# Score matmuls of a dilated attention: the keys of a query tile taken as all 1,024, or as own half, adjoining tile and every fourth key of the other half

## What is computed

```
DIL_BRANCHES = ((128, 1), (512, 4), (2048, 16))      # (window, dilation)
off  = kk[None, :] - half - qq[:, None]              # within one residue class
mask = abs(off) <= half  and  0 <= key_pos < L
out  = sum over branches of softmax(lse) * branch_out
```

## Time and profile before

| | |
|---|---|
| median of three runs | 3317.93 us |
| the profiled execution | 3315.9 us |
| its span in the trace | 3313.9 us |
| TensorE matmul busy | 3197.8 us, 96% |
| TensorE weight loads busy | 2720.6 us, 82% |
| VectorE busy | 1555.4 us, 47% |
| ScalarE busy | 936.2 us, 28% |
| GpSimd busy | 901.0 us, 27% |

### The profile page before, as it was taken

How to read it: one execution, slowest core, us unless ns; L and a number is a source line. 1 busy time by engine, 2 the same in 40 slices (tenths; PEclk the granted TensorE clock), 3 DMA queues, 4 the chain that set the end, 5 groups by cost and what they waited for, 6 DMA issues and landing times.

```text
span 3313.9 us, 42751 instructions
## 1 busy us (share of the span) xinstructions
PE 3197.8 (96%) x17492; PEld 2720.6 (82%) x17492; DVE 1555.4 (47%) x3160; ACT 936.2 (28%) x1814; POOL 901.0 (27%) x570
## 2 busy tenths in 40 slices
PE   8999999999999999999989999999999999999997
PEld 7888887888888888888778888878888888888886
DVE  6866757262333333332668667572523333333336
ACT  4433434441111111111344334444411111111112
POOL 2111112653222222222441111125522222222224
PEclk9999999999999999999989999999999999999999
DMA  3111011231111111110321110021311111111112
GB/s 143 40 56 51 20 36 64 93 127 45 39 39 39 39 39 39 39 39 32 133 72 44 53 51 20 35 82 75 127 51 39 39 39 39 38 37 36 38 56 103
DMA packets 50481, 184.27 MB, mean 56 GB/s; under 512 B 8048, under 2 KB 11760, under 8 KB 46832
## 3 DMA queue, kind: packets, MB, share of 16 engines
q1 hardware_dynamic: 47984, 173.68, 15.2%
q10 hardware_dynamic: 2304, 7.87, 0.6%
HBM read 144.81 MB, written 28.84 MB: 52 GB/s over the span
## 4 chain that ended last, share of the span: by engine, by line
PE 81%; DVE 10%; DMA 3%; issue 2%; ACT 1%; SPq 1%; POOL 1%; DVEq 0%; POOLq 0%; ACTq 0%
PE PS L1739 25%; PE PS L1741 24%; PE PS L1740 24%; PE PS L1882 3%; PE PS L1851 3%; PE PS L1866 2%; DVE PT L1507 1%; SPq L624 1%; DVE XL L1350 1%; DVE ACC L1343 1%; DMA SW<-Rq 1%; DVE SW L1400 1%; DVE YO L1343 1%; DVE ACC L1346 1%; DVE YO L1346 1%
## 5 line engine op out<-in xcount | busy, mean ns | idle before, releaser
L1739 PE MATMUL PS<-XH,WH 128*128 128x512 f32 (+1 forms) x3648 | 1327.7, 364 | 21.7 <-DVE XL L1358 5.7
L1741 PE MATMUL PS<-XH,WL 128*128 128x512 f32 (+1 forms) x3648 | 1300.6, 357 | 0.0
L1740 PE MATMUL PS<-XL,WH 128*128 128x512 f32 (+1 forms) x3648 | 1300.3, 356 | 0.0
L1739 PEld LDWEIGHTS PS<-XH,WH 128*128 128x128 f32 x3648 | 693.5, 190 | 147.4 <-issue 21.4
L1741 PEld LDWEIGHTS PS<-XH,WL 128*128 128x128 f32 x3648 | 692.4, 190 | 101.8
L1740 PEld LDWEIGHTS PS<-XL,WH 128*128 128x128 f32 x3648 | 693.5, 190 | 93.0
L794 POOL TENSOR_TENSOR WL<-RAW,WH 128x1024 fp32r<-128x1024 f32 x196 | 468.9, 2411 | 960.8 <-ACT WH L965 960.8
L817 POOL TENSOR_TENSOR SG<-SG,RS 128x512 f32<-128x512 f32 x132 | 147.9, 1121 | 997.5 <-ACT SG L1104 997.5
L1579 DVE TENSOR_TENSOR ACC<-ACC,PS 128x512 f32<-128x512 f32 (+1 forms) x480 | 286.3, 598 | 246.4 <-PE PS L1741 245.1
L1739 PE MATMUL PS<-HH,WH 128*128 128x512 f32 (+1 forms) x1056 | 379.2, 359 | 11.9 <-DVE ACC L1579 10.4
L1741 PE MATMUL PS<-HH,WL 128*128 128x512 f32 (+1 forms) x1056 | 378.7, 359 | 0.0
(11 more groups left out here) (118 smaller groups left out, 2859.8 us busy)
## 6 DMA issues: line engine op xcount, KB each, us to landing
RAW<-w_in SPq DMA_DIRECT2D x48, 512.0 KB, 3.5
RAW<-w_gate SPq DMA_DIRECT2D x44, 512.0 KB, 3.5
RAW<-w_up SPq DMA_DIRECT2D x44, 512.0 KB, 3.5
RAW<-w_down SPq DMA_DIRECT2D x44, 512.0 KB, 3.7
X<-parked SPq DMA_DIRECT2D x6, 2048.0 KB, 7.8
RAW<-w_out SPq DMA_DIRECT2D x16, 512.0 KB, 4.2
parked<-YO SPq DMA_DIRECT2D x4, 2048.0 KB, 6.5
mixed<-YB ACTq DMA_DIRECT2D x8, 640.0 KB, 2.9
```

The lines of the kernel that those rows point to most:

```text
L1739: nc.tensor.matmul(out, wh, xh, start=first, stop=False)
L1740: nc.tensor.matmul(out, wh, xl, start=False, stop=False)
L1741: return nc.tensor.matmul(out, wl, xh, start=False, stop=last)
```

## The change

The scores of a sample pair are computed in three parts instead of two quads: the 512 keys of the query's own half, the 128 keys of the adjoining tile of the other half, and the 128 stepped keys of the other half (same residue r as the queries, moving operand with a step of 4 elements). The second and third part share bank 2h + 1. The 512 columns of one bank and 256 of the next are all that is computed. The table masks, in the adjoining tile, the keys whose distance is a multiple of 4, since those are among the stepped ones; the stepped part has no key masked for being near. The two VectorE instructions now take 512 and 256 (two pieces of 128) numbers. The order of the value tiles follows: own half, adjoining tile, stepped. The table LOG grows by 6 columns. Prompt tiles and the neighbourhood blocks are as before.

```diff
-DIL_UNITS = [(i, h, 3 * (i // 4), 6) for i in range(8) for h in range(2)] + \
+DIL_UNITS = [(i, h, 4 * (i // 4), 6) for i in range(8) for h in range(2)] + \
...
-NEAR = HALF_S + P
-LOG_STEPPED = (P + 3 + NEAR, P + 3 + NEAR + P)
+LOG_BESIDE = (HALF_S + 3, HALF_S + 3 + P + 3)
+LOG_STEPPED = (LOG_BESIDE[1] + P + 3, LOG_BESIDE[1] + P + 3 + P)
...
-    near = np.arange(P + 3 + NEAR)[None, :] - P - 3 - STEP * q
-    far = [np.arange(P)[None, :] + first for first in (P, -P)]
-    stepped = [np.where((k < P + P // STEP) & (k >= -P // STEP), f(MASKED), log_count(STEP * (k - q))) for k in far]
+    own = np.arange(HALF_S + 3)[None, :] - 3 - STEP * q
+    beside = [np.arange(P + 3)[None, :] - 3 + first - STEP * q for first in (HALF_S, -P)]
+    stepped = [STEP * (np.arange(P)[None, :] + first - q) for first in (P, -P)]
     prompt = np.arange(3 * P)[None, :] - P - q
-    log = np.concatenate([log_count(near)] + stepped + [log_count(prompt)], 1)
+    log = np.concatenate([log_count(own)] + [np.where(d % STEP, log_count(d), f(MASKED)) for d in beside]
+                         + [log_count(d) for d in stepped] + [log_count(prompt)], 1)
...
-            if b not in DIL or i >= 8 or a < 5:
+            if b not in DIL or i >= 8 or a < 4:
                 return V[:, k0 + a, h, :]
             half, r = half_of(i)
+            if a == 4:
+                return V[:, 4 - half, h, :]
             return VS[0][:, r, h, :] if half == 0 else VS[1 + r // 2][:, r % 2, h, :]
...
-                    at = (P if half == 0 else 0) + 3 - r
-                    nc.vector.tensor_tensor_reduce(PR[:, u % 2, 0:NEAR], ps[:, 3 * P * half:3 * P * half + NEAR],
-                                                   LOG[:, at:at + NEAR], -1.0, 3e38, ALU.add, ALU.min,
-                                                   NM_NEAR[:, n:n + 1]).then_inc(s_near, 1)
-                    dve.wait_ge(s_near, 16 * (DIL[-1] + 1) * L + 16 * b + u + 1)
-                    nc.vector.tensor_tensor_reduce(PR[:, u % 2, NEAR:NEAR + P], stepped(ps, 1 - half, r),
-                                                   LOG[:, LOG_STEPPED[half]:LOG_STEPPED[half] + P], -1.0,
-                                                   NM_NEAR[:, n:n + 1], ALU.add, ALU.min,
+                    low, high = LOG_BESIDE[half] + 3 - r, LOG_STEPPED[half]
+                    nc.vector.tensor_tensor_reduce(PR[:, u % 2, 0:HALF_S], ps[:, 0:HALF_S],
+                                                   LOG[:, 3 - r:3 - r + HALF_S], -1.0, 3e38, ALU.add, ALU.min,
+                                                   NM_OWN[:, n:n + 1]).then_inc(s_own, 1)
+                    dve.wait_ge(s_own, 16 * (DIL[-1] + 1) * L + 16 * b + u + 1)
+                    other = slice(HALF_S, HALF_S + 2 * P)
+                    tab = LOG[:, low:2 * high - low].rearrange("p (m n) -> p m n", m=2)[:, :, 0:P]
+                    nc.vector.tensor_tensor_reduce(PR[:, u % 2, other].rearrange("p (m n) -> p m n", m=2),
+                                                   ps[:, other].rearrange("p (m n) -> p m n", m=2),
+                                                   tab, -1.0, NM_OWN[:, n:n + 1], ALU.add, ALU.min,
                                                    NM[:, n:n + 1]).then_inc(s_masked, 1)
...
-                    halves = b in DIL and i < 8
-                    if halves:
-                        k0, nkt = 0, 2 * STEP
+                    if b in DIL and i < 8:
+                        scores_halves(pair)
+                        return
...
+                def scores_halves(pair):
+
+                    half, r = half_of(units[2 * pair][0])
+                    for part, (bank, at, n) in enumerate(((0, 0, HALF_S), (1, 0, P), (1, P, P))):
+                        for m, (q, k) in enumerate(((QH, KH), (QH, KL), (QL, KH))):
+                            keys = (k[:, HALF_S * half:HALF_S * half + HALF_S],
+                                    k[:, (4 - half) * P:(5 - half) * P], stepped(k, 1 - half, r))[part]
+                            for h in range(2):
+                                own = slice(HD * h, HD * h + HD)
+                                last = nc.tensor.matmul(PS[:, 2 * h + bank, at:at + n],
+                                                        stepped(q, half, r)[own, :], keys[own, :],
+                                                        start=m == 0, stop=m == 2)
+                                if m == 2 and part == 2:
+                                    last.then_inc(s_scored, 1)
```

More of the change, by code:

```diff
@@ L438, in build @@
         STAT = place("STAT", [P, 16], offset=base + 97920)
-        NM, SM, NM_NEAR, CW = STAT[:, 0:4], STAT[:, 4:8], STAT[:, 8:12], STAT[:, 12:15]
+        NM, SM, NM_OWN, CW = STAT[:, 0:4], STAT[:, 4:8], STAT[:, 8:12], STAT[:, 12:15]
         YS = place("YS", [P, 2, P], offset=base + 97984)
@@ L491, in build @@
         s_masked = sem("masked")
-        s_near = sem("near")
+        s_own = sem("own")
         s_exped = sem("exped")
@@ L1849, in scores @@
                                 own = slice(HD * h, HD * h + HD)
-                                qs = stepped(q, *half_of(i)) if halves else q[:, i * P:(i + 1) * P]
-                                last = nc.tensor.matmul(PS[:, 2 * h + a // 4, 0:n * P], qs[own, :], k[own, keys],
+                                last = nc.tensor.matmul(PS[:, 2 * h + a // 4, 0:n * P],
+                                                        q[own, i * P:(i + 1) * P], k[own, keys],
                                                         start=m == 0, stop=m == 2)
                                 if m == 2 and a + n == nkt:
+                                    last.then_inc(s_scored, 1)
[11 more added lines that the diff above has]
+                                if m == 2 and part == 2:
                                     last.then_inc(s_scored, 1)
```

## The result

The changed kernel takes 3338.39 us (median of four runs, 3334.35 to 3340.21) against 3316.91 us of the kernel before: a ratio of 1.0066, 95% interval 1.0049 to 1.0084, so slower by 0.66%, 21.5 us. Predicted were 3333 us, +15. The two profiled spans are 3313.9 and 3335.5 us, 21.6 apart.

A forecast was written before the change was run, and what follows sets the result against it. TensorE was taken as the bound: 3315.9 us profiled, +16.3 for 33 pairs on the chain, +1 for 15 others, -1 for VectorE, gave 3332.2, so a median near 3333 us. Likeliest range 3328 to 3341 us; 8 in 10, 3319 to 3350.

The forecast's parts named there:

- The bound: In the stretches with dilated blocks, TensorE sets the time, busy 317.80 of 329 and 321.91 of 336 us.
- 6 x 0.22 = +1.32 us: On TensorE, six new 128-column steps per sample pair, each at the pace of a stepped-query load, 0.22 us.
- The end of the pair: On TensorE, last matmul start to next group's load shrinks from 0.33 to 0.21 us: -0.12 us a pair.
- 33 of the 48 sample pairs set the end: Pairs on TensorE's part of the chain, each 0.495 us longer: 33 x 0.495 = +16.3 us.
- On the 15 others a longer pair first uses up the wait that follows: Pairs off TensorE's chain: mean wait of 0.86 us absorbs most of the 0.495 us each, leaving +1 us.
- some 12: TensorE's waits for PT low in the dilated stretches were to shrink from 18 us to some 12.
- 814 + 351 ns become about 681 + 410 ns: VectorE's two masking instructions: -0.074 us a unit, -7.1 us over 96, of which -1 us counts on the chain.
- the step cost 77 ns, which is the whole gain: Bound for VectorE's masks: if two pieces cost as much extra as the step does now, nothing is saved.
- (a): Rival: stepped loads on TensorE keep up at 0.11 us, so the kernel gets faster, 3310.5 us; chance 0.10.
- (b): Rival: stepped keys fight the loads for SBUF, +1.26 us a pair, 3366 us; chance 0.14.
- (c): Rival: VectorE's slack absorbs TensorE's extra time, at most 10.4 us through the waits, near 3322 us; chance 0.14.
- half-way, 3345 us: Mark given under the rival of stepped keys fighting loads, between the forecast and that rival's 3366 us.

The follow-up runs named there:

- run 8: Changed kernel with the part over the adjoining tile done twice, same result: 3366.04 us, ratio 1.0154 to the kernel before.
- run 4: Changed kernel with the dilated blocks' queries stored by residue, so a query tile is plain, same result: 3313.26 us, 0.9989 of the kernel before.
- run 6: Changed kernel with queries stored by residue and the second mask as one run of 256 numbers (wrong table): 3315.06 us, 1.0000 of the kernel before.
- run 9: Changed kernel with queries stored by residue, repeated with more executions: 3314.54 us, 0.9995 of the kernel before.
- run 1: Changed kernel with plain queries in sample pairs, stepped keys kept (other scores): 3312.67 us, 0.9987 of the kernel before.
- run 2: Changed kernel with plain keys in the third part, queries still stepped (other scores): 3334.26 us, 1.0054 of the kernel before.
- run 5: Changed kernel with the second masking instruction as one run of 256 numbers instead of two pieces (wrong table): 3339.34 us, 1.0071 of the kernel before.
- run 11: Changed kernel with the second mask's minimum started from a constant, not the first one's result: 3340.28 us, 1.0071 of the kernel before.
- run 3: Changed kernel with both queries and third-part keys plain (other scores): 3313.53 us, 0.9992 of the kernel before.
- run 7: Kernel before, still in two quads, with only its dilated blocks' queries stored by residue: 3314.29 us, 0.9998 of the kernel before.
- the three-part form with residues: Changed kernel with the dilated blocks' queries written side by side by residue: 3313.26 us (0.9989 of the kernel before), again 3314.54 us (0.9995).

## Why the prediction was right, step by step

**The bound.** TensorE leads in these stretches: right. Extra time on it shows at 37.7 us for each us of a pair (21.5 / 0.57), and 39.5 to 42 for the next 0.70 us (run 8). Cutting it pays less: from the kernel before down to 1.56 us it is 0.17 us a pair for 0 to 4 us (runs 4, 6 and 9), 0 to 22 us for each us.

**What a short step costs.** The mechanism was right: a 128-column matmul cannot hide a load of stepped queries. Runs 1 and 2 settle it, since plain queries take the whole loss away and plain keys almost nothing. The loads of the short steps are 0.233 us apart. But the six steps together took less than "6 x 0.22 = +1.32 us": from the start of the last long matmul, 86.76, to that of the last short one, 88.00, it is 1.24 us, since the second short matmul is put only 0.06 us behind the first.

**The end of the pair** was the term that was off: "-0.12 us", a last start to next load of 0.21 us read from a pair with plain queries. It measured 0.36 us after, 0.33 with plain keys. A load that is exposed between short steps is exposed at the end too. The two sizes err in opposite ways, -0.08 us for the six steps and +0.15 for the end, so a pair grew by 0.57 us instead of 0.495. That the sum is so near is in part luck. Counted by loads: from the first to the last it is 1.85 us where it was 1.17, three loads more, +0.68, and from the last to the next group's 0.45 us where it was 0.56, -0.11. With plain keys a pair is 0.04 us shorter (run 2); the rest is the slow loads.

**The pairs that count.** "33 of the 48 sample pairs set the end" held for the kernel before. "On the 15 others a longer pair first uses up the wait that follows" was priced at 1 us; 10 of the 15 came onto the chain, and one of the 33 left it. 33 x 0.57 = 18.8 us, 42 x 0.57 = 23.9; measured 21.5, between. TensorE's waits for PT low and the sums are 15.3 us in 19, after 18.0 in 21, but over windows 39 us longer in all. Over the same work (80 to 421 and 1746 to 2087 us) they are 13.8 us in 17, still more than "some 12".

```profile
PE PS L1902 <- DVE PT L1512: 6.2, 7, 2.1
...
PE PS L1911 <- DVE YS L1486: 1.2, 2, 0.6
```

Those two lines are TensorE's waits in layer 0, 80 to 425 us, against the earlier trace rows; in layer 1, 1745 to 2100 us, they are 5.4 and 2.5 us.

**VectorE.** "814 + 351 ns become about 681 + 410 ns" was wrong, though its bound ("the step cost 77 ns, which is the whole gain") has the measured value. The reason given for the bound is wrong too: 484 ns stays in one piece (run 5) and falls to 425 with a constant start (run 11). The second mask of the kernel before has such a start as well, so of the 77 ns that the prediction gave to the step some 59 are likely the start and 18 the step (an estimate from run 11). The gain was priced at 1 us, and the time shows nothing of it (run 11).

**The rivals.** (a), loads at 0.11 us in short steps, is what plain queries do and stepped ones don't. The figure of 81 ns in the Trainium skill, "TensorE: Matmul & The Clock Gate", section on the back-to-back issue gap, is not reached here even with both operands plain: the loads of run 3 are 0.11 us apart. There two loads and two matmuls, one for each head, run side by side; but the transposes, single 128x128 matmuls with a load each, start 0.11 us apart too in the trace of the kernel before. (b), stepped keys against the loads, is refuted by runs 1 and 2: 0.04 to 0.05 us a pair, not 0.16 or more. (c), absorption, took part of it: 21.5 of 48 x 0.57 = 27.4 us are left.

**The sums.** The prediction's own terms, 3332.2 + 2.0 us, give 3334.2 and not 3333, and its "half-way, 3345 us" under (b) follows from no sum that it shows (half of +48 us gives 3342). Neither changes how the result is read.

## What to carry to other kernels

Cutting columns out of a matmul saves its stream, and each piece that is left still needs its own weight load. Before splitting one, read the pace of loads where no long matmul hides them: at 0.233 us a load, a 128-column piece costs as much as a 512-column one. A stationary operand read with a step costs little while its loads hide behind wide matmuls (0.14 us a pair, run 7, which the time doesn't show) and much once they are short. Storing it side by side when it is written takes the loss away, if the engines that write it have room. It does not turn this change into a gain: the three-part form with residues measured 0.9989 and 0.9995 of the kernel before.

## What the runs showed of the hardware

- Stepping by 16 bytes slows the stationary operand, from 0.11 us a load of 128 columns to 0.21 (start of a pair) and 0.233 (short steps), and hardly the moving one: matmuls of 128 columns stand 0.12 to 0.13 us apart instead of 0.11 (runs 1 and 3). The Trainium skill, "SBUF — State Buffer", in the part on the DMA port swizzle, has a penalty for each access to a new 16-byte line; here it bites on the load side.
- VectorE's masking instruction costs 59 ns more when its minimum starts from another instruction's result than from a constant (484 and 425 ns for 256 numbers in two pieces). With that start, two pieces cost no more than one (484 and 484 ns, run 5 and the changed kernel).
